# The up matrices of the experts issued from ScalarE's queue, gate and down from SyncE's

## What is computed

```python
hid = jax.nn.silu(xb @ w_gate[e]) * (xb @ w_up[e])
return hid @ w_down[e]
```

## Time and profile before

| | |
|---|---|
| median of 3 runs | 1320.85 us (1320.15 to 1323.23) |
| the profiled execution | 1323.06 us |
| its span | 1320.0 us |
| TensorE busy | 1142.3 us, 87% |
| VectorE busy | 510.1 us, 39% |
| ScalarE busy | 280.4 us, 21% |
| moved by DMA | 471.61 MB, 357 GB/s over the span |

### The profile page before, as it was taken

How to read it: one execution, slowest core, us unless ns; L and a number is a source line. 1 busy time by engine, 2 the same in 40 slices (tenths; PEclk the granted TensorE clock), 3 DMA queues, 4 the chain that set the end, 5 groups by cost and what they waited for, 6 DMA issues and landing times.

```text
span 1320.0 us, 17790 instructions
## 1 busy us (share of the span) xinstructions
PE 1142.3 (87%) x7341; PEld 659.7 (50%) x7341; DVE 510.1 (39%) x817; ACT 280.4 (21%) x444; POOL 56.8 (4%) x68
## 2 busy tenths in 40 slices
PE   7999999999999998789778877977787797779777
PEld 7888888878884444324323323432242252324223
DVE  6546677775443443213222222322131232213223
ACT  7445576684430000100000000000000000000000
POOL 3000011401100000000000000000000000000000
PEclk9999999999998888978888878887897888888877
DMA  9955554636658999999999999999999999999995
GB/s 321 290 189 178 158 174 149 235 128 221 256 225 340 429 432 431 430 429 433 432 433 430 430 434 431 433 432 431 430 433 434 430 433 430 432 433 432 431 429 210
DMA packets 83712, 471.61 MB, mean 357 GB/s; under 512 B 7138, under 2 KB 68176, under 8 KB 69200
## 3 DMA queue, kind: packets, MB, share of 16 engines
q1 hardware_dynamic: 83664, 470.94, 87.5%
HBM read 468.83 MB, written 2.10 MB: 357 GB/s over the span
## 4 chain that ended last, share of the span: by engine, by line
PE 53%; DMA 39%; DVE 5%; ACT 1%; issue 1%; POOL 1%; DVEq 0%; SPq 0%; ACTq 0%
DMA twin<-in_w_up 17%; DMA twin<-in_w_gate 16%; PE banks L1420 16%; PE banks L1642 9%; PE banks L1422 8%; PE banks L1689 6%; DMA twin<-in_w_down 5%; PE banks L1621 4%; PE banks L1591 4%; PE banks L1607 3%; DVE x_acc L1292 2%; PE banks L1441 1%; PE banks L1362 1%; DVE up_sb L1305 1%; POOL h_tok L510 1%
## 5 line engine op out<-in xcount | busy, mean ns | idle before, releaser
L1642 PE MATMUL banks<-twin,x_exp 128*32 128x512 f32 x1792 | 260.2, 706 | 84.9 <-DMA twin<-in_w_gate 68.4
L1292 DVE TENSOR_TENSOR x_acc<-x_acc,banks 128x512 f32<-128x512 f32 x256 | 158.7, 683 | 348.7 <-PE banks L1591 348.5
L1420 PE MATMUL banks<-hT,w_split 128*128 128x512 f32 x576 | 204.4, 400 | 0.1
L944 DVE TENSOR_TENSOR w_split<-ring,w_split 128x1024 fp32r<-128x1024 f32 x116 | 146.7, 1284 | 116.0 <-ACT w_split L631 115.7
L1642 PEld LDWEIGHTS banks<-twin,x_exp 128*32 128x32 f32 x1792 | 51.3, 119 | 243.2 <-issue 136.3
L1422 PE MATMUL banks<-hT,w_split 128*128 128x256 f32 x576 | 161.2, 280 | 0.0
L1689 PE MATMUL banks<-twin,hidT 128*32 128x512 f32 x864 | 144.9, 832 | 18.0 <-DVE hidT L1311 10.7
L631 ACT ACTIVATE w_split<-ring 128x1024 fp32r<-128x1024 f32 x116 | 121.7, 1060 | 125.2 <-PE banks L1422 125.1
L1420 PEld LDWEIGHTS banks<-hT,w_split 128*128 128x128 f32 x576 | 108.3, 188 | 25.9 <-issue 0.3
L843 ACT ACTIVATE y_item<-banks 64x512 f32<-64x512 f32 x32 | 18.9, 590 | 481.4 <-PE banks L1689 481.4
L1422 PEld LDWEIGHTS banks<-hT,w_split 128*128 128x128 f32 x576 | 108.8, 189 | 0.2
(11 more groups left out here) (238 smaller groups left out, 926.7 us busy)
## 6 DMA issues: line engine op xcount, KB each, us to landing
twin<-in_w_gate SPq DMA_DIRECT2D x28, 4096.0 KB, 32.4
twin<-in_w_up SPq DMA_DIRECT2D x28, 4096.0 KB, 32.2
twin<-in_w_down SPq DMA_DIRECT2D x27, 4096.0 KB, 32.3
ring<-in_w_in SPq DMA_DIRECT2D x20, 2048.0 KB, 9.2
ring<-in_w_down SPq DMA_DIRECT2D x10, 2048.0 KB, 18.2
ring<-in_w_out SPq DMA_DIRECT2D x8, 2048.0 KB, 8.4
ring<-in_w_gate SPq DMA_DIRECT2D x8, 2048.0 KB, 12.6
ring<-in_w_up SPq DMA_DIRECT2D x8, 2048.0 KB, 14.9
```

The lines of the kernel that those rows point to most:

```text
L944: dve.tensor_tensor(w_lo[:, k], src, w_hi[:, k].bitcast(F32), ALU.subtract).then_inc(lo_ready, 1)
L1292: dve.tensor_tensor(dst, dst, b_comb[n][:, :], ALU.add).then_inc(acc_done, 1)
L1420: pe.matmul(dst[:, 0:2 * PW], stationary[:, 0, cols], moving.rearrange("p s n -> p (s n)"), start=(k == 0 and cc == 0), stop=False)
L1642: ins = pe.matmul(dst[SLOTS * j:SLOTS * (j + 1), :], x_exp[:, c, cols], weights[:, cc * F:(cc + 1) * F], start=(c < 4), stop=(c >= KC - 4))
```

## The change

From the fifth item on SyncE leaves out the up matrices, wait and DMA both. ScalarE issues them instead: in the step of item i, after the copy of the gate sums, it waits for the same count of `piece_used` and issues up of item i + 1. It does so in the steps of items 3 to 30; the ups of items 0 to 3 stay with SyncE as halves, and further items are as before. Buffers, semaphores, counts and bytes are the same. SyncE's queue keeps gate and down in their order.

```diff
--- before.py
+++ after.py
@@ -427,6 +427,8 @@
                     for part, whole in enumerate((w_gate_p, w_up_p, w_down_p)):
                         j = twin_of(k, part)
                         width = F if part < 2 else D
+                        if part == 1 and n_extra is None:
+                            continue
 
                         sp.wait_ge(piece_used, q * PER_QUAD + 2 * (3 * k + part) - 6)
                         if apart(q, k, part):
@@ -817,7 +819,7 @@
             load_table(ACT.Silu)
 
 
-            def item_step(q, k):
+            def item_step(q, k, further_quad=False):
                 i = q * QI + k
                 begins = first_quad(q) and k == 0
 
@@ -825,6 +827,12 @@
                 if not begins:
                     act.wait_ge(fold_full, i)
                 act.activation(gate_sb[:, :], b_gate[:, :], ACT.Copy).then_inc(gate_out, 1)
+                if not further_quad and not (first_quad(q) and k < QI - 1) and not (closing_quad(q) and k == QI - 1):
+
+                    j = twin_of((k + 1) % QI, 1)
+                    act.wait_ge(piece_used, i * PARTS + 2)
+                    act.dma_start(twin[j][:, :].rearrange("p (c n) -> p c n", n=F),
+                                  w_up_p[i + 1]).then_inc(piece_in[MOE_ORDER[2 * j]], 16)
 
                 act.wait_ge(gate_folded, i + 1)
                 if not begins:
@@ -849,7 +857,7 @@
                         item_step(q, k)
                     else:
                         with act.If(n_extra > (q - QUADS) * QI + k):
-                            item_step(q, k)
+                            item_step(q, k, True)
 
             quad(0)
             with act.Fori(1, QUADS - 1) as q:
```

## The result

The changed kernel takes 1329.83 us (median of 7 runs, 1326.35 to 1331.39) against 1322.4 us of the kernel before (7 runs, 1320.15 to 1323.23). The ratio is 1.006, 95% interval 1.0051 to 1.0069: 7.4 us slower, 6.7 to 9.1 by the interval. The forecast was +9.1. The profiled execution took 1329.0 us and has a span of 1326.3, 6.3 more than before.

A forecast was written before the change was run, and what follows sets the result against it. The expert phase was taken as bound by moving 4 MB matrices back to back. All else counting 0, 9.71 - 0.64 = +9.07 us at the end took 1320.85 to 1329.9 us; range 1320 to 1335.

The forecast's parts named there:

- Part 1: SyncE drops the up wait and 28 issues of 0.33 us, 9 us in all; its time is free: 0 us.
- Part 2: ScalarE issues up behind the gate copy, 0.6 us later; about 0.4 us per issue, covered by idle time: 0 us.
- Part 3: Both queues get half the engines; up lands 19.4 us after issue, gate one matrix later; 0 us in the middle.
- The end: At item 31, gate lands with one matrix left behind it instead of two: +9.07 us.
- first term: Gate of item 31 lands at 1291.08 us instead of 1281.37: +9.71 us.
- second term: TensorE's wait for up of item 31 goes, as up is already there: -0.64 us.
- term that I kept at the old value: TensorE's clock in item 31, old mix kept; old chain from gate to end of span 38.63 us, including 0.64 waiting.
- bound for the pace: Up and down of the last item at TensorE's quick pace would give -3.2 us; not put in the sum.
- The entry: Around item 4, matrices shift among themselves by up to 10 us, but no gap arises: 0 us.
- Order of issue kept: Rival: one line for both issuers, so up still runs behind down and gate; 1320.9 us, chance 0.16.
- Fuller engines: Rival: two queues close gaps between matrices, 4.6 us; 1325.3 us with the late gate, 1316.3 without; chance 0.11.
- Slower mixed streams: Rival: turning between two matrices costs 7.9 us besides the late end, 1338 us; chance 0.06, shared with TensorE's cover going.

The follow-up runs named there:

- e5: Kernel before, with ScalarE issuing all matrices in the old order from up of item 5 on (81 issues): 1321.62 us against 1321.68.
- e1: Kernel after, with up of the last item alone given back to SyncE: 1322.72 us against 1321.68 of the kernel before, ratio 1.0006.
- e7: Kernel before, with down instead of up issued by ScalarE, from item 5 on: 1326.47 us against 1321.68, ratio 1.0030.
- e2: Kernel before, with only up of the last item issued by ScalarE: 1330.61 us against 1321.68, ratio 1.0068.
- e3: Kernel before, all on SyncE's one queue, with up of the last item issued ahead of its gate: 1330.11 us, ratio 1.0062.
- e4: Kernel before, with all 84 matrices from item 4 on issued by ScalarE in the old order: 1337.25 us, ratio 1.0119.
- e9: As e7, but down of the last item as one DMA with 32 KB rows, not two with 16 KB: 1331.19 us against 1321.98, ratio 1.0064.
- e10: Up issued by ScalarE when down is used up, no longer after gate, from item 5 on: 1631.54 us, ratio 1.2335 to the kernel before.
- e8: Kernel before, all on SyncE, with gate and up of the last item loaded as two halves each: 1318.13 us against 1321.68, ratio 0.997.

## Why the prediction was right

**The number.** The ratio says +6.7 to +9.1 us, and the forecast of +9.07 lies at the upper end of it. That the median came within 0.1 us of the forecast (1329.83 against 1329.9) is luck: the kernel before was taken at 1320.85 us, 1.55 below its median of seven runs, and the change at 1.6 us too much.

**What bounds the kernel.** Right. The rate from 450 to 1290 us is 431 GB/s before, after and in e5; no moved issue of the middle shows in the time (e1, e5).

**Part 1, SyncE freed.** Worth nothing, as said.

**Part 2, ScalarE's issue.** The cost of nothing holds (e5, 81 issues). The working was wrong in one point: the issue does not wait for the copy ahead of it to end. When TensorE is done with gate, both start together, here in the step of item 28:

```profile
1208.33 0.60 ACT L829 ACTIVATE gate_sb<-banks 128x512 f32<-128x512 f32 x1 [11.53 <-PE banks L1650]
1208.34 0.35 ACTq L834 DMA_DIRECT2D twin<-in_w_up  x1
```

So the 0.6 us of delay is 0.01 here. In the items of the loop, 24 of the 28, some register instructions stand between, and it is 0.15 (copy at 860.12, issue at 860.27). Neither shows in the time.

**Part 3, the share.** The result holds: the new queue is served beside the old one. By what I read it from doesn't. I took q8's low rate per engine for the sign of a shared engine. The queues of the kernel after do share, and their packets are as quick as before: 117.44 MB in 20.6% of 16 engines' 1326.3 us is 26.9 GB/s for q10, 25.0 for q1, beside 25.5 for q1 alone before. A shared queue doesn't have slow packets here, it has fewer of them; q8's rows say nothing of it. Half each came out of turns by packets (126 and 126), which are as large for all whole matrices, and not out of q8's speed, and e7 shows the share move away from half when the rows differ. Up took 23.5 us to land and not 19.4. For up of item 30 the trace has 3 us without a packet ahead of its rows, 126 of its 128 rows from 1242 to 1260 us, and the landing at 1263.9. The working had no such term; up is in before gate all the same, so gate's lateness stays.

**The end.** Right in kind and place: e2 and e3 produce the loss with one matrix, with and without a second queue, and e1 takes it away. In size, the first term was 9.71 us and measured 8.52; about one microsecond of the difference is that the loads of this execution ended earlier. The second term, 0.64 us for the wait that goes, is there. The term that I kept at the old value is TensorE's pace behind G(31): 38.0 us forecast, 36.4 measured. Most of it is the first half of up of item 31. It took 3.59 us at a granted clock of 0.52 before, and 1.92 us at 1.00 after (windows over that half, columns as in rows 2):

```profile
1291.08:1294.67 3.59, 3.59 (x20) 0.66 (x20) 0.00 (x0) 0.00 (x0) 0.00 (x0) 0.52 0.96 411
1299.08:1301.00 1.92, 1.92 (x21) 0.48 (x20) 0.00 (x0) 0.55 (x2) 0.00 (x0) 1.00 0.12 43
```

The two terms, 1.2 and 1.6 us, are the gap between +9.07 and the 6.3 by which the two profiled spans differ. How much of either is in the medians isn't shown. The bound for the pace (-3.2) stood in the text; half of it came.

**The entry.** Zero in the time, as said, but closer than it looked: TensorE waited 2.6 us for down of item 3, which up of item 4 had begun to overtake, and began item 4 at 509.92 us instead of 504.46. The middle took these 5.5 us up, as the engines stayed full. In e4 they did not, and it cost 15.6 us.

**The rivals.** Order of issue kept: falls by the 23.5 us to landing and by e2. Fuller engines: the slices from the 14th on are 428 to 435 without the last, before 429 to 434. Slower mixed streams: none that e1's interval could show. The Trainium skill's sentence that each engine takes the queues in turn by packets ("DMA: Bandwidth & Descriptors", "Queues, rings and completion order") is borne out by 126 to 126 packets in the kernel after, 44 to 46 in e7 and 32 to 32 in e9. Its rule that spreading DMAs over issuers only saves issue time ("Rules for kernel authors") holds for the bandwidth here, but not for the time of the kernel.

**Open.** What happens in the 3 us between an issue and its first packet, no run shows. Whether the remaining 1 us of e1 is real can't be told from its interval.

## What to carry to other kernels

A second DMA queue was no more bandwidth here, where the engines are full; it was another order of landing, and the later-issued transfer overtook what the first queue still held. Before moving a load, write down for the beginning and the end of the stream what lands before and after what, and what the engines still have to compute behind each landing; in the middle four buffers hid it all here (e1, e5), but only with the issue made early (e10). Where the stream's end is the bound, split the last loads so that computing keeps pace with them (e8, 3.6 us here).

## What the runs showed of the hardware

- Two hardware queues share the 16 engines packet by packet, and a packet here is a row (q10 of the kernel after: 4032 packets for 28 matrices, 144 each, 128 rows and 16 more): 126 packets to 126 in 18 us (after), 44 packets to 46 with 1.31 MB to 0.75 MB (e7, rows of 32 and 16 KB), 32 to 32 with 1.05 MB each (e9, equal rows). Loading down whole and not as two halves with half the row cost 4.4 us more (+9.2 in e9, +4.8 in e7); the number of DMAs changed with the rows.
- No packet of a matrix shows in the first 2.5 to 3 us behind its issue on ScalarE's queue: issued at 1238.98, 1269.08 (after) and 1259.45 (e2), none until 1242, 1272 and 1262.
- ScalarE starts a DMA whose wait is satisfied 0.01 us (step of item 28, kernel after) to 0.15 us (items of the loop) after the start of an ACTIVATE of 0.60 us ahead of it, and not behind its end.
- TensorE's pace behind gate of item 31 differs between kernels with the same work. To the end of the span it took 38.63 us at a mean granted clock of 0.77 (before), 36.41 at 0.84 (after), and 34.78 at 0.88 where it had not waited for any matrix of the item (e1). A wait for a matrix alone does not decide it: a half ran in 1.92 us behind a wait of 3.61 (815.13 before), and the first half of down of item 31 took 3.42, 3.19 and 3.11 us in the three kernels with no wait for a matrix.
